# Order of the head products and the decay rows of a hybrid decoder layer on TensorE

## The reference, cut to what matters

```
xn = rms_norm(x);  proj = xn @ w_in          # q | k | v | z | xBC | dt
attention: 8 query heads of 64, 2 key heads (4 query heads each), window 128
  s = q k^T * scale, masked to the band;  p = softmax with a sink;  o = p v
state space (SSD), chunks of 128, 8 heads, 2 groups:
  a_cum = cumsum(dt * a, axis=time)
  decay[l, s] = exp(a_cum[l] - a_cum[s])  for s <= l
  y = (C B^T * decay) (x dt)  +  C h * exp(a_cum)  +  d_skip x
h = x + concat(o, gated y) @ w_out
y = h + top-2 of 32 experts (chosen within one of 4 groups)
```

## Time and profile before

| what | value |
|---|---|
| runs shown, us | 939.4, 941.13, 941.3 (median 941.13) |
| profiled execution, span from first to last instruction | 939.0 us |
| PE busy | 823.0 us (88%) |
| DVE busy | 479.8 us (51%) |
| ACT busy | 258.4 us (28%) |
| POOL busy | 147.8 us (16%) |
| HBM moved | 146 GB/s over the span |

### The profile page before, as it was taken

One profiled execution on the slowest core, in us unless ns is written; L12 is line 12 of the kernel. 1 busy time (PEld: TensorE's weight loads), 2 busy tenths in 40 slices (PEclk: granted clock), 3 DMA queues, 4 the chain that ended last, 5 costly groups with the idle time before them and its releaser, 6 DMA issues.

```text
span 939.0 us, 13161 instructions
## 1 busy us (share of the span) xinstructions
PE 823.0 (88%) x4478; PEld 583.9 (62%) x4478; DVE 479.8 (51%) x1357; ACT 258.4 (28%) x607; POOL 147.8 (16%) x238
## 2 busy tenths in 40 slices
PE   5999999999999999999999995298599999999910
PEld 2877577676686695785786532243388887777800
DVE  1766585675765766766765731175412222222236
ACT  1251351431531621522513412141022222221200
POOL 0011001010101110110110110023133333333200
PEclk9999999999999999999999997557689999999965
DMA  7940100100100101001001001564589998887268
GB/s 254 313 119 2 68 1 2 69 1 1 69 0 23 46 0 59 10 0 69 0 0 50 8 18 62 164 253 134 184 276 332 338 331 292 315 292 289 81 227 335
DMA packets 56354, 119.43 MB, mean 127 GB/s; under 512 B 15198, under 2 KB 27246, under 8 KB 56286
## 3 DMA queue, kind: packets, MB, share of 16 engines
q1 hardware_dynamic: 43590, 89.31, 27.9%
q0 software_dynamic: 9216, 16.93, 4.9%
q10 hardware_dynamic: 3504, 12.68, 3.5%
HBM read 103.52 MB, written 33.11 MB: 146 GB/s over the span
## 4 chain that ended last, share of the span: by engine, by line
issue 46%; PE 21%; DMA 14%; SPq 7%; POOL 5%; DVE 3%; ACT 1%; POOLq 1%; DVEq 1%; ACTq 0%
DMA w_arena<-in_w_down 8%; PE bank L1689 8%; PE bank L1695 4%; SPq L408 3%; SPq L404 3%; POOL rstd L1273 3%; DMA w_arena<-y_dram 3%; PE bank L1405 3%; PE bank L1418 2%; DMA w_arena<-in_w_in 1%; DVE cv L891 1%; POOL xde L1304 1%; POOL xd L1301 1%; DMA pT<-v_new 1%; POOLq L1272 1%
## 5 line engine op out<-in xcount | busy, mean ns | idle before, releaser
L1418 PE MATMUL bank<-w_arena,xT 128*128 128x512 f32 (+3 forms) x464 | 174.8, 533 | 3.2 <-DMA w_arena<-in_w_in 3.2
L1418 PEld LDWEIGHTS bank<-w_arena,xT 128*128 128x128 f32 (+1 forms) x464 | 79.4, 175 | 88.7 <-issue 83.1
L1689 PEld LDWEIGHTS bank<-w_arena 128*128 128x128 f32 x992 | 116.9, 195 | 26.0 <-issue 20.6
L1689 PE MATMUL bank<-w_arena 128*128 128x128 f32 x992 | 119.1, 279 | 7.4 <-DMA w_arena<-in_w_down 6.4
L1435 PE MATMUL bank<-xT,w_arena 128*128 128x128 f32 x1024 | 116.8, 275 | 0.0
L1435 PEld LDWEIGHTS bank<-xT,w_arena 128*128 128x128 f32 x1024 | 116.1, 192 | 0.5
L1271 POOL TENSOR_TENSOR stat<-stat,eps 128x1 f32<-128x1 f32 (+4 forms) x35 | 6.8, 193 | 447.1 <-ACT junk L557 160.0
L1208 DVE TENSOR_TENSOR w_arena<-w_arena,bank 128x128 f32<-128x128 f32 x32 | 9.2, 288 | 112.8 <-ACT w_arena L692 112.8
L1695 PE MATMUL bank<-w_arena 128*128 128x512 f32 x124 | 60.4, 609 | 0.7 <-DVE w_arena L1208 0.7
L1449 PE MATMUL bank<-w_out_sb,aT 128*128 128x512 f32 x128 | 57.7, 593 | 0.0
L1449 PE MATMUL bank<-w_out_sb,gT 128*128 128x512 f32 x128 | 57.5, 592 | 0.0
(11 more groups left out here) (303 smaller groups left out, 1215.1 us busy)
## 6 DMA issues: line engine op xcount, KB each, us to landing
w_arena<-in_w_gate SPq DMA_DIRECT2D x31, 512.0 KB, 4.8
w_arena<-in_w_up SPq DMA_DIRECT2D x31, 512.0 KB, 6.3
w_arena<-in_w_down SPq DMA_DIRECT2D x31, 512.0 KB, 16.0
w_arena<-in_w_in SPq DMA_DIRECT2D x4, 2048.0 KB, 11.4
w_arena<-y_dram SPq DMA_DIRECT2D x16, 512.0 KB, 10.6
x<-in_x_prompt SPq DMA_DIRECT2D x8, 512.0 KB, 4.0
h_dram<-x ACTq DMA_DIRECT2D x8, 512.0 KB, 2.7
t_dram<-t ACTq DMA_DIRECT2D x8, 512.0 KB, 3.0
```

What stands on the lines that cost most here:

```text
L1418: ins = pe.matmul(out, xT[:, k, 0:n], w_in[:, k, cols], start=k == 0, stop=k == KC - 1)
L1689: ins = pe.matmul(out[:, a * P:(a + 1) * P], gu[:, a, k, :], xgT[w % 2][:, k, :], start=k == 0, stop=k == KC - 1)
```

## The change

The scores are issued key head by key head in turn, so that neighbouring products use disjoint halves of the array's rows, and the wait for `tt` moves ahead of all of them. DVE takes the banks in the new order 3, 5, 4, 6. The value products take the two key heads in turn within each block of keys, so that neighbouring products use disjoint halves of the array's columns. The decay rows become transposes of a repeated column of `cum`, behind a wait for `cum`.

```diff
-                for i, b in enumerate((3, 4, 5, 6)):
+                for i, b in ((0, 3), (2, 5), (1, 4), (3, 6)):
                     now(dve, f"sc{i}", tile)
...
-                for i, b in enumerate((3, 4, 5, 6)):
-                    if i == 2 and not first:
-                        now(pe, "tt", tile - 1)
+                if not first:
+                    now(pe, "tt", tile - 1)
+                for half in range(2):
                     for j in range(2):
-                        kv, r = (2 * i + j) // REP, (2 * i + j) % REP
-                        rr = slice(kv * HD, kv * HD + HD)
-                        ins = pe.matmul(bank[b][:, j * 256:(j + 1) * 256], qT[rr, r, :], kT[rr, :, :].rearrange("p a b -> p (a b)"),
-                                        start=True, stop=True)
-                    ins.then_inc(S[f"sc{i}"], 1)
+                        for kv in range(NKV):
+                            rr = slice(kv * HD, kv * HD + HD)
+                            ins = pe.matmul(bank[3 + 2 * kv + half][:, j * 256:(j + 1) * 256], qT[rr, 2 * half + j, :],
+                                            kT[rr, :, :].rearrange("p a b -> p (a b)"), start=True, stop=True)
+                            if j == 1:
+                                ins.then_inc(S[f"sc{2 * kv + half}"], 1)
...
+                now(pe, "cum", tile)
                 for hh in range(SH):
-                    ins = pe.matmul(bank[5 + hh // 4][:, (hh % 4) * P:(hh % 4 + 1) * P], dt[:, 4, hh:hh + 1].to_broadcast([P, P]), tri,
-                                    start=True, stop=True)
+                    ins = pe.transpose(bank[5 + hh // 4][:, (hh % 4) * P:(hh % 4 + 1) * P], cum[:, 0, hh:hh + 1].to_broadcast([P, P]), ident)
...
-                for kv in range(NKV):
-                    for blk in range(2):
+                for blk in range(2):
+                    for kv in range(NKV):
                         ins = pe.matmul(bank[4][kv * HD:(kv + 1) * HD, :], v[:, blk, kv * HD:(kv + 1) * HD],
```

## The result

The changed kernel was faster, and by more than forecast: 934.71 us as the median of four runs (932.67 to 937.96), beside 941.06 for the kernel before in four runs (939.4 to 941.3). The ratio is 0.9939, interval 0.9915 to 0.9962, so 3.6 to 8.0 us; forecast were 3.5. A second, longer measurement, of 12 runs, gave 935.14 beside 939.80: ratio 0.9951, 0.9935 to 0.9968, that is 4.6 us with 3.0 to 6.1.

The account below looks back on a forecast made before the run. Warm tiles were taken as bound by a chain through DVE and PE, not PE alone. Gains of 1.15 + 0.9 + 0.58 + 0.9 = 3.5 us gave 935.5 profiled, 937.6 with 2.1 carried over; range 935.5 to 941.2.

Parts of the forecast that it names:

- the warm tiles gain nothing: Tiles 1, 3, 4 and 6: the decay rows' 0.9 us becomes PE's wait for the division; worth 0, at most 0.06.
- scores and values: Scores: same end after ACT's copy, gain 0, at worst 1.3 us lost; value products: already paired, gain 0.
- tile 0 and tile 7: Tile 0: decay rows' 0.9 and scores' 0.25 count, 1.15 us; tile 7, PE late by 1.60: 0.9 us.
- In tile 2, 0.9 of 1.19; in tile 5, 0.58 of 0.64: Two loop tiles at the low clock, PE late by 1.19 and 0.64: decay rows gain 0.9 and 0.58 us.
- C: More tiles see the low clock after xn: 0.6 us a tile, 2.4 over forecast, 940.0; chance 0.12.
- A: Every tile: PE bounds it, the new orders pair all scores and values; 35 us gain, 906; chance 0.03.
- B: Scores no longer pair where heads alternate: end 1.3 us later, 3 us in 7 tiles, 940.6; chance 0.08.
- D: Decay rows: transposing a repeated column costs as much as the product; only 0.25 us left, 940.9; chance 0.06.
- E: PE's idle time ahead of the scores lowers the clock for scores and router: 3 us a tile, 961; chance 0.06.

Follow-up runs that it names:

- The later selection: Router's selection, rank product and ACT's part moved behind the gated norm: added to the whole change 930.96 us (0.9905), to the kernel before 938.36 (0.9986).
- the product in the gap: One unread 128x512 product added between router and transposes of xn: kernel before 934.65 us (0.9953), decay rows alone 934.25 (0.9935), whole change 932.64 (0.9925).

## Why the prediction was right in its mechanism and wrong in one size

**Right: the warm tiles gain nothing.** In tiles 1 to 6 they are 65.55 to 65.87 us in both kernels, and PE waits for the division in the changed one. The later selection turned this argument into a measurement: only without DVE's work in the way are the 0.9 us worth 0.9 us.

**Right: scores and values.** The scores' end stayed with ACT's copy. Head by head behind the same wait gave the same time (0.9954 and 0.9951), and the values' order gave none (1.0014). The scores' order alone measured -0.17%, with zero at the edge of its interval; whether a part of it is real stays open.

**Right: tile 0 and tile 7.** Tile 0 lost 1.18 us (1.15 forecast). Tile 7, in the profiles without falls, lost 65.68 - 64.85 = 0.83 (0.9 forecast). The forecast put this down to a fall; it holds without one, too. The next rows are then the sample tokens', `xT` takes 0.29 us there instead of 1.29, and DVE has nothing to hide PE's time behind:

```profile
515.19 0.29 DVE L734 TENSOR_TENSOR xT<-bank,norm_sb 128x32 f32<-128x32 f32 x2 [2.87 <-PE bank L1405]
```

**Wrong in size: the step "In tile 2, 0.9 of 1.19; in tile 5, 0.58 of 0.64".** For the tiles of the loop at the low clock it put 0.9 + 0.58 = 1.5 us into the sum, from the one set of falls that one profile showed, and carried this to the median. But the falls come in other tiles in each run, and at another moment of the tile. In the two profiles, with two falls in the loop on either side, this term measured 1.8 us. Beside the same tiles without a fall (the rows of the table with the product), the old kernel lost 67.47 - 65.84 and 67.03 - 65.72, together 2.94, and the new one 66.15 - 65.70 and 66.28 - 65.59, together 1.14.

Over the runs it can only be estimated, from the kernels with the product in the gap: 4.4 less 2.4 us by the ratios, 5.4 less 2.5 by the medians, so 2.0 to 2.9 us, with the uncertainty named there. (Tile 7's falls stand in it; its gain in a warm state does not.) With tile 0's 1.18 and tile 7's 0.83 the sum is 4.0 to 4.9, and the second measurement gave 4.6. Whether the price of a fall or the number of the falls was put too low by more, these runs don't show.

What is left of a fall in the new kernel is 0.45 to 0.8 us in the loop (66.15, 66.28, 66.51, 66.27). That is not only PE's lateness, 0.42 in tile 4 and nothing in tile 1, but DVE's as well. The forecast named DVE's lateness under C, with 0.6 a tile, which is near.

The rest of the way from 4.6 to the first measurement's 6.35 lies within the spread. In 29 runs of the kernel before, which lie between 935.7 and 944.0, time and mean clock move together (correlation -0.80, 0.6 us for each 0.001 of the clock), so four runs on either side can't tell such a difference. The forecast's range allowed for this spread at its upper end only: 934.71 lies 0.8 us below its lower end, while the second measurement's ratio, taken of 941.1, gives 936.5, inside it.

**The rivals.** A is out: no tile came near 4 us of gain. B is out: 16 records in 2.00 us. D is out: 8 records in 1.04. E is out: no stretch at 0.50 lies between the scores and the transposes of `xn` in the two profiles of the changed kernel. C was half right: how often the clock falls did decide a part, and in the decay rows alone it took the whole gain. But the falls cost the whole change less than before, and its reasons failed. The moved wait with its idle time did not lower the mean clock by itself (0.927 for the order of the scores alone, 0.925 before). The Trainium skill (TensorE: Matmul & The Clock Gate, Part 4, "PE-mode transpose") has it that transposes don't count as PE work as products do; the run with each row transposed twice doesn't bear that out (0.928 against 0.926).

**Open.** Why the decay rows alone meet so many falls, and the whole change does not, isn't settled. The instructions alone don't decide it: the two profiles of the changed kernel show the falls in tiles 1, 4 and 7, with the first scores at 49.09, and in tiles 3 and 6, with the first scores at 48.63. So it proves little that the doubled rows met them in the tiles of before; the mean clock over their runs is the better evidence. That the falls depend on the time at which a tile comes is a guess which no run here tests by itself.

## What to carry to other kernels

Before pricing a shorter stage, look for the engine that arrives next: here 0.9 us of PE in each warm tile came back as a wait for DVE, and the same 0.9 us became a gain once the selection was out of DVE's way. Where one profile shows a few stretches at the low clock, treat their number and place as a sample and price them over runs; filling the gap ahead of them with one cheap product measures them, and may be the better change (0.5% here, as much as the whole change). Read the spacing of records before counting on an order that pairs products, for they may run in pairs already.

## What the hardware showed that was not expected

- Work that nobody reads can save time. One product of 1.10 us a tile in an idle gap took 4.4 us off the kernel before.
- Products on disjoint halves ran beside each other without being issued in turn: 64 records of 512 columns took 15.5 us in either order, and scores issued head by head took 2.94 us for 16 records where 3.5 would be single file. For the scores issuing in turn shortens this to 2.00, for the values it changes nothing.
- The place of the falls moves with small edits and from run to run: tiles 2, 5 and 7 before; 1, 4 and 7 or 3 and 6 in two runs of the changed kernel; 3, 6 and 7 with the order of the scores alone; or five tiles, with one fall of 6.8 us, after an edit that took PE work away.
